# Block 0's first tiles multiplied by unnormalised x, rstd put in at emptying, and a new order of the first loads

## The chip, the cores and the metric

One core of a Trainium2 chip. The metric is the device time of one execution in microseconds, the median over runs. An execution has five engines at work: TensorE (PE), VectorE (DVE), ScalarE (ACT), GpSimd (POOL) and SyncE (SP), the last of which issues all DMAs here.

## The reference, cut to what matters

A layer takes 4096 prompt frames and 32 sample frames of width 1024, normalises each row, and projects it by W_in to 3584 columns. Two groups of 512 channels are made from the projection, both with causal convolutions along time, then mapped back by W_out and added to x.

```
hn   = x * rsqrt(mean(x * x) + 1e-6) * norm_g
proj = hn @ w_in                       # 1024 -> 3584
h, b, c, z, a, g, zb = split(proj)     # 512 columns each
out_a = b * conv3(c * h) * silu(z)
v     = a * sigmoid(g)
out_b = silu(layer_norm(conv31(v) + bias)) * silu(zb)
y     = rms_norm(x + concat(out_a, out_b) @ w_out)
```

rsqrt(...) is one number per row (frame), called rstd below. The frame is the column of a tile here, since the kernel keeps x transposed. Because rstd is a factor of the whole frame, it may stand before or after the product with W_in.

## The kernel before, in words

The frames are cut in 9 blocks of 460 columns (block 0 has 12 columns of padding and the sample's 32 frames in front). Every fp32 product is made of three: each operand is split in a high and a low part (fp32r), and high times high, high times low and low times high are added in PSUM (`split_product`, L1929; its matmuls are L1933 to L1935). A tile is 128 output channels by one block, 8 chunks of 128 input channels, so 24 matmuls.

The projection goes in 5 units of 14 periods. Unit 0 (periods 0 to 13) covers blocks 0 and 1 directly. Period n belongs to one pair of weight tiles (`ORDER`, L36): "ga" (sigmoid gate g and value a), "zz" (two tiles of zb), "hc", "bz". Its four tiles are t = 0, 1 for block 0 and t = 2, 3 for block 1. `FIRST_TILES` (L65) lists the first eight: periods 0 and 1 for block 0, then periods 0 and 1 for block 1, then period by period. Later units use a Strassen scheme for pairs of blocks, so in unit 0 the weights are also summed (POOL, `weight_sums`, L986), split, and written to HBM as forms.

What each engine does in unit 0:

- SP (L810 to L836): loads x of block 0 and 1, the gain norm_g, weight groups 0, 1 and 2; then in each period rows and x of block 2 and on (`load_row`, `load_st`), stores, weights of period n + 2 (`load_w`, L671), forms of period n + 1 (`store_forms`, L681). It issues in this order and waits in this order.
- ScalarE (L1339 to L1387): squares of x (`first_square`), mean square (`first_mean_square`), high parts of the weights (`weight_high`, L1214) and of x (`first_x_high`, L1230), and the evacuation of gate tiles through sigmoid or silu (`evacuate`, L1255) from PSUM to `sets`.
- VectorE (L1770 to L1797): sums the squares (`first_sums`, L1500), multiplies x by gain and rstd (`first_x_scale`, L1512, rstd read from PSUM), low parts of x and of weights (`first_x_low`, L1523; `weights_low`, L1531), then in each period some taps of the 31-tap convolution (`tap`, L1689), the emptying of the value tiles (`empty_banks`: `multiply_in` L1605, `gate_b` L1653), the low parts of the next weights, `finish`, more taps. The number of taps per period is a written-out quota (`tap_quota`, L150), 10 in most.
- TensorE (L2072 to L2087): mean squares as products with ones (`first_statistics`, L1939), the rstd spread over 128 partitions (`first_rstd`, L1947), ten warm-up matmuls, then the tiles. The first two tiles are made by halves (`standing_part`, L1961). Tile k uses PSUM bank k mod 6, and waits until tile k - 6 is emptied (`wait_evacuated`, L476).
- POOL (L1112 to L1126): rstd by a power (`x_row_rstd`, L951), then per period sums of weights and their low parts (`sums_low`, L1002).

```
            first_sums(0)
            first_sums(1)
            first_x_scale(0, range(HALF))
...
            for n in range(1, II):
                taps(TAPS_BEFORE[n])
                empty_banks(n - 1)
                if n + 1 < II:
                    weights_low(n + 1)
                finish(n - 1)
...
                taps(TAPS_AFTER[n])
```

## Time and profile before

| What | Before |
|---|---|
| median of 3 runs | 1566.16 us (1564.45 to 1568.77) |
| the profiled execution, its own time | 1561.36 us |
| span of its instructions | 1559.6 us |
| PE busy | 1537.6 us, 99% |
| DVE busy | 1262.9 us, 81% |
| ACT busy | 537.6 us, 34% |
| POOL busy | 578.4 us, 37% |
| DMA queue 1, share of 16 engines | 68.8% |

The span runs from the first to the last instruction of the program; the profiled execution's own time is 1.8 us longer. Times in a timeline are microseconds from the span's start. Each row of a timeline merges equal neighbours: start, time covered, engine, line, operation, output<-inputs, form, count, and in brackets how long the engine was idle before and who ended that. PEclk is the granted clock of TensorE as the records give it; they begin with the first change, so the column says 1.00 before that too.

### The profile page before, as it was taken

The numbers are of one execution on the slowest core, as the hardware profiler recorded it, in microseconds if no ns is written. First come the engines' busy times: TensorE is split into PE (matmuls) and PEld (weight loads), VectorE is DVE, ScalarE is ACT, GpSimd is POOL, SyncE is SP. The second block draws the span as 40 slices with busy tenths as digits, with TensorE's granted clock in tenths as the row PEclk, the third lists the DMA queues.
The fourth block names the chain that finished last, engine by engine and source line by source line (L and its number), as shares of the span: only waits on it lengthen the run. The fifth ranks groups of instructions, "written<-read, shape, count | busy, mean of one in ns | idle before, by whom it ended". The sixth has DMA issues, their size and how long they took to land. (4 is left out here: it accounts for less than half of the span.)

```text
span 1559.6 us, 19243 instructions
## 1 busy us (share of the span) xinstructions
PE 1537.6 (99%) x7244; PEld 1358.4 (87%) x7244; DVE 1262.9 (81%) x1175; ACT 537.6 (34%) x780; POOL 578.4 (37%) x494
## 2 busy tenths in 40 slices
PE   6999999999999999999999999999999999999998
PEld 6999999988888888888888888888898888888886
DVE  7699799998878998869798888789896677787853
ACT  5443433332242333332253312234533323323221
POOL 2766969112313121132221141146964233332320
PEclk9999999999999999999999999999999999999999
DMA  4987978788987789897779877757645433445441
GB/s 164 337 320 279 339 266 317 261 276 287 292 276 241 232 250 301 288 289 247 233 231 298 255 239 246 215 174 221 203 121 192 162 126 138 168 162 188 142 142 69
DMA packets 109648, 358.03 MB, mean 230 GB/s; under 512 B 16676, under 2 KB 20644, under 8 KB 105976
## 3 DMA queue, kind: packets, MB, share of 16 engines
q1 hardware_dynamic: 109560, 356.86, 68.8%
q8 instruction: 55, 0.90, 0.2%
q14 instruction: 33, 0.27, 0.0%
HBM read 263.02 MB, written 93.79 MB: 229 GB/s over the span
## 5 line engine op out<-in xcount | busy, mean ns | idle before, releaser
L1704 DVE SCALAR_TENSOR_TENSOR ps<-v,conv_b_taps,ps 128x920 f32<-128x920 f32 (+2 forms) x580 | 630.9, 1088 | 17.8
L1933 PE MATMUL ps<-xf,w_ring 128*128 128x460 f32 (+1 forms) x1624 | 602.8, 371 | 1.0 <-issue 0.8
L1935 PE MATMUL ps<-xf,w_ring 128*128 128x460 f32 (+1 forms) x1624 | 602.6, 371 | 0.0
L1934 PE MATMUL ps<-xf,w_ring 128*128 128x460 f32 (+1 forms) x1624 | 600.8, 370 | 0.0
L1933 PEld LDWEIGHTS ps<-xf,w_ring 128*128 128x128 f32 x1624 | 305.4, 188 | 35.2 <-issue 2.1
L1934 PEld LDWEIGHTS ps<-xf,w_ring 128*128 128x128 f32 x1624 | 305.4, 188 | 34.0
L1935 PEld LDWEIGHTS ps<-xf,w_ring 128*128 128x128 f32 x1624 | 304.9, 188 | 34.2
L1268 ACT ACTIVATE sets<-ps 128x460 f32<-128x460 f32 x168 | 92.9, 553 | 488.7 <-PE ps L1935 488.5
L1074 POOL TENSOR_TENSOR sets<-sets 128x460 f32<-128x460 f32 x42 | 56.2, 1337 | 414.9 <-ACT sets L1268 414.9
L1933 PE MATMUL ps<-w_out_split,mixed 128*128 128x512 f32 x528 | 206.0, 390 | 0.0
L1934 PE MATMUL ps<-w_out_split,mixed 128*128 128x512 f32 x528 | 205.7, 390 | 0.0
L1935 PE MATMUL ps<-w_out_split,mixed 128*128 128x512 f32 x528 | 205.5, 389 | 0.0
L1933 PEld LDWEIGHTS ps<-w_out_split,mixed 128*128 128x128 f32 x528 | 99.1, 188 | 21.2 <-DVE mixed L1765 0.5
L1935 PEld LDWEIGHTS ps<-w_out_split,mixed 128*128 128x128 f32 x528 | 99.1, 188 | 20.8
L1934 PEld LDWEIGHTS ps<-w_out_split,mixed 128*128 128x128 f32 x528 | 99.1, 188 | 20.5
L1477 ACT ACTIVATE ps<-h_rows 128x1024 f32<-128x1024 f32 x32 | 33.0, 1030 | 200.0 <-DVE h_rows L1851 200.0
L945 POOL TENSOR_TENSOR row_mean_sq_eps<-row_mean_sq,rms_eps 128x1 f32<-128x1 f32 x32 | 8.4, 264 | 228.4 <-ACT ps L1477 228.3
L1014 POOL TENSOR_TENSOR w_ring<-w_ring_f,w_ring 128x512 fp32r<-128x512 f32 x56 | 74.8, 1355 | 43.6 <-ACT w_ring L1228 43.6
L1933 PE MATMUL ps<-xf 128*128 128x448 f32 (+1 forms) x224 | 82.7, 369 | 0.0
L1935 PE MATMUL ps<-xf 128*128 128x448 f32 (+1 forms) x224 | 82.6, 369 | 0.0
L1934 PE MATMUL ps<-xf 128*128 128x448 f32 (+1 forms) x224 | 82.2, 367 | 0.0
L971 POOL TENSOR_TENSOR x_raw<-x_raw,rstd_spread 128x460 f32<-128x460 f32 x56 | 66.5, 1220 | 40.2 <-DMA rstd_spread<-rstd_spill 40.2
(166 smaller groups left out, 1650.2 us busy)
## 6 DMA issues: line engine op xcount, KB each, us to landing
w_ring<-weight_forms SPq DMA_DIRECT2D x294, 512.0 KB, 5.3
x_rows_again<-in_x_prompt SPq DMA_DIRECT2D x32, 512.0 KB, 4.3
out_y_prompt<-h_rows SPq DMA_DIRECT2D x32, 512.0 KB, 3.0
weight_forms<-xf SPq DMA_DIRECT2D x7, 2048.0 KB, 13.3
weight_forms<-w_ring SPq DMA_DIRECT2D x7, 2048.0 KB, 14.7
w_ring_f<-in_w_in SPq DMA_DIRECT2D x56, 256.0 KB, 3.1
xf_f<-in_w_in SPq DMA_DIRECT2D x26, 512.0 KB, 9.0
x_row<-in_x_prompt SPq DMA_DIRECT2D x28, 460.0 KB
```

The source lines that it names most:

```text
L945: pool.tensor_tensor(mean_sq[0:rows, r:r + 1], ssq[0:rows, r:r + 1], add, ALU.add).then_inc(h_ms, 1)
L971: pool.tensor_tensor(part, part, spread[:, 0:TB], ALU.mult).then_inc(x_scaled, 1)
L1014: pool.tensor_tensor(ring[:, slot, 1, :], ring_f32[:, slot, 1, :], ring[:, slot, 0, :].bitcast(F32), ALU.subtract).then_inc(late_lo, 1)
L1074: pool.tensor_tensor(sets[:, s, QC, :], sets[:, s, QC, :], sets[:, s, QD, :], ALU.add).then_inc(c22_made, 1)
L1268: act.activation(sets[:, n % 2, quarter, :], ps[:, bank, 0:TB], ACT.Copy).then_inc(copied, 1)
L1477: act.activation(out_pair(2)[0:rows, :], hrow[0:rows, s, :], ACT.Square, scale=RMS_SCALE, accum_out=ssq[0:rows, s:s + 1]).then_inc(h_sumsq, 1)
L1704: dve.scalar_tensor_tensor(dst, window, wb[:, j, k:k + 1], part, ALU.mult, ALU.add).then_inc(taps_done, 1)
L1933: pe.matmul(out, ahi, bhi, start=(start and x == 0), stop=False, skip_group_check=goes_on)
L1934: pe.matmul(out, ahi, blo, start=False, stop=False, skip_group_check=goes_on)
L1935: mm = pe.matmul(out, alo, bhi, start=False, stop=(stop and x == len(terms) - 1), skip_group_check=goes_on)
```

## The change

Block 0's x is no longer normalised before its first tiles. ScalarE makes the high part of x times gain (`raw_x_high`), VectorE the low part (`raw_x_low`), and the tiles (0,0), (0,1), (1,0) and (1,1) are multiplied with these. Block 1 is normalised first (`TURN` swaps the two blocks in the counts of the semaphores). The statistics of block 1 and its rstd come between the halves of the first two tiles, those of block 0 between the halves of tiles (0,2) and (0,3). Then ScalarE copies block 0's rstd from PSUM to `spread`, VectorE multiplies three tiles by it into `sets` (`raw_tile`), ScalarE applies sigmoid or silu in place (`gate_raw`), and the fourth, a's tile of period 0, gets it by a multiplication of its gate (`raw_gate`). After that block 0's x is scaled and split as before (`first_x_scale(0)`, `first_x_low(0)`), into the same buffers, for periods 2 to 13. The tiles (2,0) and (2,1) are made by halves. Squares of block 0 go to `sets` instead of a slot of `xf`. The first DMA is the gain; weight group 0 is loaded before block 1's x. POOL makes block 1's rstd, group 0's sums and low parts, block 0's rstd, then group 1's. The warm-up has 14 matmuls and starts when the first low part of x is there. Group 2's high and low weights are made before the loop over periods, and the emptying of period 0 too.

```diff
             def spread_rstd(w, b):
                 sp.wait_ge(rstd_out, 16 * stat_count(w, b))
+                if (w, b) == (1, 0):
+                    sp.wait_ge(x0_tiles, 3)
...
+            sp.dma_start(gain[:, :], A["norm_g"]).then_inc(gain_in, 16)
             for x in range(2):
                 src = A["xT"][0, :, x].rearrange("p (k t) -> p k t", t=TB)
                 sp.dma_start(st[:, x, :, :], src).then_inc(first_x_in[x], 16)
-            sp.dma_start(gain[:, :], A["norm_g"]).then_inc(gain_in, 16)
+            load_w(0)
             for x in range(2, 4):
...
-            load_w(0)
             load_w(1)
...
-            x_row_rstd(0, 1)
-            x_row_rstd(1, 2)
-            pool.wait_ge(x01_lo, 4)
+            x_row_rstd(1, TURN[1] + 1)
             weight_sums(0)
-            pool.wait_ge(x01_lo, 8)
             sums_low(0)
+            x_row_rstd(0, TURN[0] + 1)
             weight_sums(1)
...
+            def raw_x_high(k):
+                act.wait_ge(gain_in, 16)
+                act.wait_ge(first_x_in[k // HALF], 16)
+                act.activation(standing_x(0, 0, k, k + 1)[:, 0, :], st[:, k // HALF, k % HALF, :], ACT.Copy,
+                               scale=gain[:, k:k + 1]).then_inc(x0_raw_hi, 1)
+            def gate_raw(n, t):
+                part = sets[:, n, QUARTER[TILE_QUARTER[t]], PAD:TB]
+                act.wait_ge(x0_tiles, 2 * n + t + (1 if n == 0 else 0))
+                act.activation(part, part, FUNC[kind(n)]).then_inc(act_made, 1)
             def first_x_high(b, r):
-                act.wait_ge(x01_scaled, KC * b + 2 * r + 2)
+                act.wait_ge(x01_scaled, KC * TURN[b] + 2 * r + 2)
+                if b == 0:
+                    act.wait_ge(tile_done, TILE_AT[1, 1])
...
+            for k in range(6):
+                raw_x_high(k)
+            weight_high(0, 0)
+            raw_x_high(6)
+            raw_x_high(7)
+            weight_high(0, 1)
+            first_square(1, 0)
+            first_square(1, 1)
+            weight_high(1, 0)
+            weight_high(1, 1)
+            act.wait_ge(ready0, 7)
+            first_mean_square(1)
             first_square(0, 0)
             first_square(0, 1)
...
+            first_x_high(1, 0)
+            first_x_high(1, 1)
+            weight_high(0, 2)
+            first_x_high(1, 2)
+            weight_high(0, 3)
+            first_x_high(1, 3)
             first_mean_square(0)
...
+            act.wait_ge(first_spread, TURN[0] + 1)
+            act.activation(spread[:, 0:TB], ps[:, FIRST_BANK[0], 0:TB], ACT.Copy).then_inc(x0_rstd, 1)
+            gate_raw(0, 0)
             evacuate(0, 2)
+            gate_raw(1, 0)
+            gate_raw(1, 1)
+            weight_high(2, 0)
+            weight_high(2, 1)
             weight_high(1, 2)
             weight_high(1, 3)
+            for r in range(4):
+                first_x_high(0, r)
...
+            def raw_x_low(ks):
+                for k in ks:
+                    dve.wait_ge(x0_raw_hi, k + 1)
+                    dve.scalar_tensor_tensor(standing_x(0, 1, k, k + 1)[:, 0, :], st[:, k // HALF, k % HALF, :],
+                                             gain[:, k:k + 1], standing_x(0, 0, k, k + 1)[:, 0, :].bitcast(F32),
+                                             ALU.mult, ALU.subtract).then_inc(x0_raw_lo, 1)
+            def raw_tile(n, t):
+                dve.wait_ge(x0_rstd, 1)
+                dve.wait_ge(tile_done, TILE_AT[n, t])
+                dve.tensor_tensor(sets[:, n, QUARTER[TILE_QUARTER[t]], PAD:TB], ps[:, bank_of(n, t), PAD:TB],
+                                  spread[:, PAD:TB], ALU.mult).then_inc(x0_tiles, 1)
...
+            dve.wait_ge(gain_in, 16)
+            raw_x_low(range(6))
+            weights_low(0, [0])
+            raw_x_low(range(6, KC))
+            weights_low(0, [1])
+            first_sums(1)
+            weights_low(1)
+            first_x_scale(1, range(HALF))
+            first_x_low(1, range(2))
+            first_x_scale(1, range(HALF, KC))
+            first_x_low(1, range(2, 4))
             first_sums(0)
-            first_sums(1)
+            raw_tile(0, 0)
+            raw_tile(1, 0)
+            raw_tile(1, 1)
+            raw_gate()
+            dve.wait_ge(x0_gate, 1)
+            empty_banks(0)
+            weights_low(2)
             first_x_scale(0, range(HALF))
...
             for n in range(1, II):
                 taps(TAPS_BEFORE[n])
-                empty_banks(n - 1)
-                if n + 1 < II:
-                    weights_low(n + 1)
+                if n > 1:
+                    empty_banks(n - 1)
+                    if n + 1 < II:
+                        weights_low(n + 1)
                 finish(n - 1)
...
             pe.wait_ge(ready0, 7)
-            first_statistics(0)
-            first_rstd(0)
-            first_statistics(1)
-            for _ in range(10):
+            pe.wait_ge(x0_raw_lo, 1)
+            for _ in range(14):
                 pe.matmul(ps[:, 5, 0:P], ident[:, :], ident[:, :], start=True, stop=True)
...
+            by_halves(0, (0, 1), {2: (first_statistics, 1), 3: (first_rstd, 1)})
+            standing_tile(1, 0)
+            standing_tile(1, 1)
+            by_halves(0, (2, 3), {1: (first_statistics, 0), 2: (first_rstd, 0)})
+            standing_tile(1, 2)
+            standing_tile(1, 3)
+            by_halves(2, (0, 1), {})
+            for n, t in [(2, 2), (2, 3)] + [(n, t) for n in range(3, II) for t in range(4)]:
                 standing_tile(n, t)
```

## Rows read from the trace of the kernel before

**Rows 1.** The page's part on busy time: engine, busy us, share, instructions.

```profile
PE 1537.6 (99%) x7244; PEld 1358.4 (87%) x7244; DVE 1262.9 (81%) x1175; ACT 537.6 (34%) x780; POOL 578.4 (37%) x494
```

**Rows 2.** The timeline of TensorE, 0 to 28 us.

```profile
12.70 1.82 PE L1944 MATMUL ps<-ones,xf_f 128*115 128x1 f32 x8 [12.70 <-DVE xf_f L1510]
16.17 2.06 PE L1953 MATMUL ps<-ident,x_rstd_columns 115*128 115x115 f32 x8 [1.65 <-POOL x_rstd_columns L956]
18.02 1.69 PE L1944 MATMUL ps<-ones,w_ring_f 128*115 128x1 f32 x8
19.56 4.54 PE L2078 MATMUL ps<-ident 128*128 128x128 f32 x20
23.83 0.48 PE L1933 MATMUL ps<-xf 128*128 128x448 f32 x1
...
26.39 1.04 PE L1953 MATMUL ps<-ident,x_rstd_columns 115*128 115x115 f32 x8
27.20 0.45 PE L1933 MATMUL ps<-xf 128*128 128x448 f32 x1
```

**Rows 3.** The timeline of VectorE, 174 to 189 us.

```profile
174.21 0.58 DVE L1662 TENSOR_TENSOR conv_a_acc<-ps,conv_a_acc 128x416 f32<-128x416 f32 x1
...
187.73 0.64 DVE L1618 TENSOR_TENSOR v<-ps,sets 128x460 f32<-128x460 f32 x1 [6.25 <-ACT sets L1262]
```

**Rows 4.** L1933's products by stretch: stretch and length, PE busy (count), PEclk, DMA, GB/s.

```profile
23.80:84.10 60.30, 35.55 (x96) 1.00 0.70 260
...
23.80:177.90 154.10, 91.41 (x248) 1.00 0.79 290
```

**Rows 5.** The timeline of VectorE, the first 62 us.

```profile
7.34 1.12 DVE L1506 TENSOR_TENSOR xf_f<-xf_f 128x920 f32<-128x920 f32 x1 [7.34 <-ACT xf_f L1182]
...
18.32 2.51 DVE L1520 SCALAR_TENSOR_TENSOR x_raw<-x_raw,gain,ps 128x460 f32<-128x460 f32 x4 [1.28 <-PE ps L1953]
20.74 1.22 DVE L1534 TENSOR_TENSOR xf<-xf_f,xf 128x1024 fp32r<-128x1024 f32 x1
21.88 2.14 DVE L1526 TENSOR_TENSOR xf<-x_raw,xf 128x920 fp32r<-128x920 f32 x2
...
59.16 1.25 DVE L1701 TENSOR_SCALAR ps<-v,conv_b_taps,conv_b_bias_sb 128x938 f32<-128x938 f32 x1
```

**Rows 6.** VectorE's waits, 59.2 to 175 us: us in total, times, longest.

```profile
DVE w_ring L1534 <- ACT w_ring L1222: 1.1, 1, 1.1
```

**Rows 7.** The timeline of SP's DMA issues, 0 to 2 us and 57 to 65 us.

```profile
1.68 0.42 SPq L813 DMA_DIRECT2D gain<-in_norm_g  x1
...
57.84 1.06 SPq L641 DMA_DIRECT2D x_raw<-in_xT  x1
...
64.43 0.80 SPq L679 DMA_DIRECT2D xf_f<-in_w_in  x2
```

**Rows 8.** The timeline of ScalarE, the first 50 us and near 90 us.

```profile
5.57 1.74 ACT L1182 ACTIVATE xf_f<-x_raw 128x1840 f32<-128x1840 f32 x1 [3.54 <-DMA x_raw<-in_xT]
7.83 1.74 ACT L1182 ACTIVATE xf_f<-x_raw 128x1840 f32<-128x1840 f32 x1 [0.53 <-DMA x_raw<-in_xT]
...
14.78 1.99 ACT L1222 ACTIVATE xf<-xf_f 128x1024 fp32r<-128x1024 f32 x2
...
28.59 1.28 ACT L1262 ACT_TABLE_LOAD   x1
...
89.28 1.24 ACT L1201 ACTIVATE x_raw<-x_raw,gain 128x460 f32<-128x460 f32 x2
```

**Rows 9.** The timeline of POOL, the first 50 us.

```profile
14.96 1.15 POOL L956 TENSOR_TENSOR x_rstd_columns<-x_mean_square_eps,minus_half 115x4 f32<-115x4 f32 x1 [13.20 <-ACT x_mean_square_eps L1187]
...
42.13 4.77 POOL L1006 TENSOR_TENSOR xf<-xf_f,xf 128x1024 fp32r<-128x1024 f32 x2 [5.24 <-DVE xf L1526]
```

**Rows 10.** The timeline of VectorE at two places where POOL is at work.

```profile
76.37 3.49 DVE L1534 TENSOR_TENSOR w_ring<-xf_f,w_ring 128x1024 fp32r<-128x1024 f32 x2
...
159.08 5.30 DVE L1650 SCALAR_TENSOR_TENSOR conv_a_acc<-u,conv_a_taps,conv_a_acc 128x910 f32<-128x910 f32 x2
```

More of the change, by code:

```diff
@@ L373, in build_program @@
         first_spread = sem("first_rstd_spread")
+        x0_raw_hi = sem("x0_raw_hi")
+        x0_raw_lo = sem("x0_raw_lo")
+        x0_rstd = sem("x0_rstd_copied")
+        x0_tiles = sem("x0_tiles_times_rstd")
+        x0_gate = sem("x0_gate_times_rstd")
         x01_scaled = sem("x01_scaled")
@@ L989, in weight_sums @@
                 if g == 1:
-                    pool.wait_ge(first_stat, 2)
+                    pool.wait_ge(first_stat, TURN[1] + 1)
                 for f in range(2):
@@ L1514, in first_x_scale @@
                 dve.wait_ge(gain_in, 16)
-                dve.wait_ge(first_spread, b + 1)
+                dve.wait_ge(first_spread, TURN[b] + 1)
                 for k in ks:
@@ L1965, in standing_part @@
                 for r in rs:
-                    if n == 0:
-                        pe.wait_ge(x01_lo, 4 * b + r + 1)
+                    if n == 0 and b == 0:
+                        pe.wait_ge(x0_raw_lo, 2 * r + 2)
+                    elif (n, b) in ((0, 1), (2, 0)):
+                        pe.wait_ge(x01_lo, 4 * TURN[b] + r + 1)
                     terms = []
@@ L2072, in _, with by_halves @@
             pe.wait_ge(ready0, 7)
-            first_statistics(0)
-            first_rstd(0)
-            first_statistics(1)
-            for _ in range(10):
+            pe.wait_ge(x0_raw_lo, 1)
+            for _ in range(14):
                 pe.matmul(ps[:, 5, 0:P], ident[:, :], ident[:, :], start=True, stop=True)
-            for rs in (range(2), range(2, 4)):
-                for t in range(2):
-                    pe.wait_ge(w_lo_w, t + 1)
-                    standing_part(0, t, rs)
-                    if t == 0 and rs[0] == 0:
-                        first_rstd(1)
-            for n, t in FIRST_TILES[2:] + [(n, t) for n in range(2, II) for t in range(4)]:
+            def by_halves(n, ts, between):
+                for x, (rs, t) in enumerate((rs, t) for rs in (range(2), range(2, 4)) for t in ts):
+                    if t < 2:
+                        pe.wait_ge(w_lo_w, 2 * n + t + 1)
+                    if rs[0] == 0 and 4 * n + t >= 6:
+                        wait_evacuated(pe, *divmod(4 * n + t - 6, 4))
+                    standing_part(n, t, rs)
+                    if x in between:
+                        between[x][0](between[x][1])
+            by_halves(0, (0, 1), {2: (first_statistics, 1), 3: (first_rstd, 1)})
[6 more added lines that the diff above has]
+            for n, t in [(2, 2), (2, 3)] + [(n, t) for n in range(3, II) for t in range(4)]:
                 standing_tile(n, t)
```

49 lines of the change are left out of this document (15 added, 34 removed).

## The prediction

> **What bounds the kernel now.** I read the page's busy shares first, then TensorE's waits, then the four engines' timelines of the first 60 us, then how far TensorE had come at set times. TensorE is busy 99% of the span [rows 1]; the view of its waits lists four, and only the first is long: 12.7 us for the sums of block 0's squares. Two more stretches come before the first useful product: the rstd of block 0 (16.17 us) and ten warm-up products, 20 passes from 19.56 us. The first product of the projection starts at 23.83 us [rows 2]. From there TensorE runs on almost without a break, so the end moves by what TensorE's first product gains, less what is put between products, less every new stall. A lead at the start is worth something only if no other engine's deadline uses it up.
>
> The tightest deadline comes much later, on VectorE. A tile's PSUM bank is used again six tiles on, and for tile 1 of a period VectorE must have emptied it. In period 6 VectorE does that with L1662, ending at 174.8 us (174.21 + 0.58) [rows 3], and the 32nd tile, which waits for it, starts at 177.9: 248 of L1933's products, eight to a tile, had started by then [rows 4]. That is 3.1 us of room. Between its first tap at 59.16 us [rows 5] and 174.8 VectorE waits only 1.1 us for ScalarE at the weights of period 5 [rows 6]. So a late first tap stays late there, less at most 1.1 us.
>
> **The start.** norm_g's DMA goes first, 0.42 us of issue [rows 7], and x of block 0 lands that much later: ScalarE began on its halves at 5.57 and 7.83 us [rows 8], so now at 6.0 and 8.2. The two halves are 2.26 us apart for 920 KB, so a 512 KB weight tile costs 1.26: the first weights land at 9.5 and 10.7. Block 1's x slips behind them to 13.0 and 15.2.
>
> ScalarE multiplies x by gain at 0.57 us a chunk (two in 1.24, one 0.67 [rows 8]). VectorE has chunk 0's low part at 7.4, pitch 0.61 [rows 5]. Weight high takes 1.05 (the second of two is done 1.99 after the first begins), low 1.22 [rows 5, 8]: ready at 11.9, the second tile at 14.2. TensorE starts 14 warm-ups at 7.4; 20 passes took 19.56 to 23.83, 0.2135 each [rows 2], so 28 take 6.0 and end at 13.4. **First product: 13.4 us, against 23.83: 10.4 us earlier.** Nothing it needs is later than that.
>
> What moves in between products: two statistics and one more rstd. The rstd (8 passes) took 26.39 to 27.20 among products, against 1.85 from 16.17 to 18.02 in front of them [rows 2]. The statistics took 1.54 (18.02 to 19.56) in that slower stretch; among products between 0.8 and 1.5, I take 1.0, as it is of the rstd's kind. Together 2.8 us.
>
> The clock: before, the products' rate doubled just where the warm-ups ended, after TensorE had been at work from 16.17 on, 7.7 us; warm-up passes of 128 columns came every 0.2135 us, the rate of the lower level, 1.2 GHz, and the rstd at 26.39 took less than half of the first. Now 6.0 us of work stand ahead of the first product, so up to 1.7 us of products run at half rate: 0 to 0.9 us, I take 0.4. The Trainium skill (TensorE: Matmul & The Clock Gate, "What's actually happening") says that the lower level is the default and activity releases it; by it all of the second level's gain might come earlier or later than I say, which the rise just at 23.9 neither confirms nor refutes.
>
> **Chain to block 0's rstd.** A tile is 4.94 us (19 tiles in the 93.8 us between two counts [rows 4]), a half 2.47. TensorE: three halves to 20.8, statistics of block 1 (its sums are done at 20.0: two squares of 1.74 [rows 8], three adds of 1.12 and one half as wide, 0.6 [rows 5]), a half, rstd to 25.1 (POOL's power 1.15 [rows 9] is hidden by the half), two tiles of pair 1 to 34.9, two halves to 39.8. VectorE from 25.1: eight scalings 4.9 (four in 2.51), four low parts 4.3 (two in 2.14), 0.7 of waiting for ScalarE, sums of block 0 4.0 [rows 5]: 39.0 at best. POOL's sums of weight group 0, which now start when the rstd of block 1 is made (23.1), run beside these. Beside POOL two low parts took 3.49 where twice 1.22 is 2.44 [rows 10]; a meeting costs VectorE 1.05. I take two, 41.1. **TensorE stalls 1.4 us** (0 to 3). Statistics to 42.2, a half, rstd at 45.5, the last half to 48.0.
>
> ScalarE copies the rstd (0.6, near the 0.57 pitch of the gain), VectorE multiplies three tiles (0.58 each, as 416 columns took [rows 3]). ScalarE loads its table (1.28 [rows 8]) before the sigmoid, done at 47.9, so the tile that needs the bank, at 48.0, doesn't wait. VectorE: raw gate, v's three pieces to 49.8. ScalarE: a second table, two silus of 0.55 to 0.6 and weight group 2's first high part, 51.7. VectorE: two low parts of weights, 54.0; then block 0's real x, which before was done at 18 to 30 us, now lies here: eight scalings 4.9, four low parts 4.3, a cast. That is 63.3 with nobody in the way; POOL's low parts of group 1 (2.4 each [rows 9]) and sums of group 2 meet two of the four, 1.05 each and a little for the lengths. **First tap about 64.7 us, 5.5 us later than 59.16.** Bounds: with no meeting at all 61.8 (2.6 late, the stall gone too), with six meetings 68.2 (9 late).
>
> **What is queued behind the moved steps.** SP loads block 2's x into the same buffer and now waits for block 0's low parts, until about 64.6; before, that DMA went at 57.84 [rows 7]. Behind it stand the state's store, group 3's weights and group 2's forms. Group 3's weights went out at 64.43 before [rows 7], so they slip 1 to 2 us, less than VectorE's own 5.5. ScalarE in order: group 2's high parts moved ahead of the taps, nothing of TensorE behind them. POOL's rstd of block 0 ahead of group 1's sums costs 1.15, hidden by ScalarE's wait. The head's lead hides none of this.
>
> **The sum.** TensorE reaches period 2 at 57.9 plus about 1.5 of waiting for block 0's low parts, against 64.4 (84.1 less four tiles [rows 4]): some 5 us ahead. Then group 3's low weights, first at 77.6 (76.37 plus half of 3.49 [rows 10]), come 5.5 late, at 83.1, where TensorE stood at 84.1 before with its 13th tile [rows 4]: the lead is down to 1. In period 6 VectorE is 5.5 - 1.1 = 4.4 late and the room was 3.1: **+1.3 us** for everything after. Then VectorE waited 6.25 us of its own before, at 187.73 [rows 3], so its lateness ends there; TensorE's doesn't, since it has no idle time to give up. The profiled execution took 1561.36 us by the clock of the runs; 1.3 more is 1562.7. The median of the three runs shown is 4.8 above it, and the forecast is made against the median: 1566.16 + 1.3 = 1567.4. Bounds of the first tap (2.6 to 9 late) give -1.6 to +4.8. Below 0.3%, 4.7 us, a change can't be told from none.
>
> **Rivals.** (a) *The lead is kept*, 1559.2. TensorE ends 7 us earlier (10.4 - 2.8 - 0.4, as if no stall came). VectorE would have to be done in period 6 at least 3.9 us earlier than before, some 8 less than I have; for a gain over 4.7 it must be 1.6 early, some 6 less. For it: VectorE's ops with two inputs in SBUF are stretched by POOL in these periods (a pair of low parts by 1.05; two steps of group A's convolution took 5.30 where the first tap, a little wider, took 1.25 [rows 5, 10]): five pairs and two convolutions, some 11 us in all. If a late VectorE meets POOL idle, that goes. Against: ScalarE must split the same weights first, and POOL's low parts follow it at once, so the late VectorE meets those instead. 0.17.
>
> (b) *VectorE late enough to be slower*, 1572. The same port, the other way: six meetings in the first 65 us (9 late, +4.8), and one more in periods 2 to 6, +1.1. It decides from a first tap at about 68 us. For it: every low part of x and every add of squares now lies in POOL's busy time; the price of one is 1.05 [rows 10]. Against: scalings read PSUM and ran at 0.61 beside POOL. 0.17. The Trainium skill (SBUF - State Buffer, "Who interferes with whom") says that a VectorE instruction with two inputs in SBUF contends with a GpSimd one that reads SBUF, and that one blocks for the other's whole length; 3.49 for 2.44 is in that direction. By it a meeting with a POOL instruction of 2.4 could cost 2.4.
>
> (c) *The start doesn't come earlier*: weights or x held up behind each other so that the first product is at 18 or later. The time is the forecast's all the same, since VectorE decides; it has no chance of its own.
>
> **How the numbers follow.** Forecast 0.66, its own range 1564.5 to 1571; (a) 0.17; (b) 0.17. Faster 0.17, same 0.66, slower 0.17. The range for 8 in 10 reaches half into both rivals: 1560.5 to 1572.
>
> **What would show it.** Right: first product near 13.4, TensorE's products at full rate by 15; a wait of 1 to 2 us before block 0's statistics; first tap near 64.7; TensorE waiting a few us for group 3's low weights near 78 to 83, and again for VectorE's conv_a_acc or v pieces in periods 4 to 6; the 32nd tile near 179. Wrong: a first tap before 62 with no TensorE waits after 90 (then (a)), or one after 68, or waits of TensorE for DMA or ScalarE, which I have none of.

## The result, and the profile after

The changed kernel takes 1573.58 us (median of 6 runs, 1572.37 to 1575.81), the kernel before 1565.87 in the runs beside it: a ratio of 1.0051 with a 95% interval of 1.0038 to 1.0064. It is slower by 0.5%, where a change too small to be told from none was predicted (1567.4 us). Its profiled execution took 1573.64 us, with a span of 1571.9. That is 12.3 us more than the profiled span of before (1559.6), but that execution took 1561.36 us, 4.5 less than the median of 1565.87; by the medians the change costs 7.7.

The page's busy shares of the changed kernel, to be held against [rows 1]:

```profile
PE 1544.8 (98%) x7252; PEld 1362.2 (87%) x7252; DVE 1277.6 (81%) x1187; ACT 542.4 (35%) x789; POOL 569.3 (36%) x494
```

TensorE does eight matmuls more, all of them warm-ups, and is busy 7.2 us longer: work done at half clock, mostly. VectorE has twelve instructions more and 14.7 us more of busy time, of which the new instructions (eight low parts, three tiles and one gate) explain about half.

The view of TensorE's waits, those of 1 us and more (us in total, times, longest):

```profile
PE ps L2143 <- DVE xf L1566: 9.2, 1, 9.2
PE ps L1998 <- DVE w_ring L1586: 5.6, 1, 5.6
PE ps L1998 <- DVE xf L1558: 1.8, 2, 1.6
PE ps L1998 <- POOL mixed L1110: 1.1, 1, 1.1
PE ps L2009 <- DVE sets L1542: 1.1, 1, 1.1
```

The 12.7 us for block 0's squares became 9.2 for the first low part of x. The new long one is 5.6 us for the low part of a weight tile. TensorE's timeline shows where each comes:

```profile
9.24 6.26 PE L2143 MATMUL ps<-ident 128*128 128x128 f32 x28 [9.24 <-DVE xf L1566]
22.66 1.65 PE L2009 MATMUL ps<-ones,w_ring_f 128*115 128x1 f32 x8
26.70 1.04 PE L2018 MATMUL ps<-ident,x_rstd_columns 115*128 115x115 f32 x8
43.65 1.85 PE L2009 MATMUL ps<-ones,sets 128*115 128x1 f32 x8 [1.10 <-DVE sets L1542]
49.49 1.04 PE L2018 MATMUL ps<-ident,x_rstd_columns 115*128 115x115 f32 x8
91.08 0.74 PE L1998 MATMUL ps<-xf,w_ring 128*128 128x448 f32 x1 [5.64 <-DVE w_ring L1586]
```

The first product starts at 15.21 us, 8.6 earlier than the 23.83 of [rows 2]. The row at 91.08 is the first product of period 3; the products behind it start every 0.37 us, those of the kernel before there every 0.20. TensorE's clock is at its lower level there. The view by stretch (stretch and length, busy us with count for PE, PEld, DVE, ACT, POOL, then the granted clock):

```profile
40.00:47.00 7.00, 5.90 (x27) 5.14 (x26) 3.52 (x4) 0.26 (x1) 1.13 (x2) 0.93 1.00 425
47.00:49.00 2.00, 2.00 (x7) 1.74 (x6) 0.00 (x0) 0.00 (x0) 1.92 (x2) 0.50 0.80 328
49.00:60.00 11.00, 11.00 (x55) 9.64 (x55) 6.74 (x11) 8.98 (x11) 4.23 (x4) 0.98 0.01 4
91.00:98.00 7.00, 6.92 (x20) 6.17 (x21) 6.86 (x7) 3.65 (x6) 0.00 (x0) 0.55 0.80 253
98.00:110.00 12.00, 12.00 (x61) 10.95 (x60) 11.82 (x11) 5.04 (x6) 10.22 (x6) 1.00 0.85 350
```

The clock records of the trace show that it fell twice to 1.2 GHz: from 46.04 for 3.41 us, after a wait of 1.1 us and eight passes of one column; and from 90.41 for 6.83 us, 5.0 us into the wait of 5.64. The first fall cost 1.7 us: the half tile from 45.35 to 49.49 took 4.14 us, and the same products took 2.48 in the kernel before. The second cost 2.9 (the experiment a_fill, below).

VectorE's timeline from block 0's rstd to its first tap and near 90 us:

```profile
51.16 1.69 DVE L1574 TENSOR_TENSOR sets<-ps,rstd_spread 128x448 f32<-128x448 f32 x3 [7.57 <-ACT rstd_spread L1385]
...
59.09 2.50 DVE L1552 SCALAR_TENSOR_TENSOR x_raw<-x_raw,gain,ps 128x460 f32<-128x460 f32 x4
61.50 4.31 DVE L1558 TENSOR_TENSOR xf<-x_raw,xf 128x920 fp32r<-128x920 f32 x2
65.74 2.50 DVE L1552 SCALAR_TENSOR_TENSOR x_raw<-x_raw,gain,ps 128x460 f32<-128x460 f32 x4
68.16 3.29 DVE L1558 TENSOR_TENSOR xf<-x_raw,xf 128x920 fp32r<-128x920 f32 x2
71.37 1.31 DVE L1846 CAST mean_w<-mean_w_f 128x128 fp32r<-128x128 f32 x1
72.60 1.25 DVE L1753 TENSOR_SCALAR ps<-v,conv_b_taps,conv_b_bias_sb 128x938 f32<-128x938 f32 x1
...
84.99 4.91 DVE L1756 SCALAR_TENSOR_TENSOR ps<-v,conv_b_taps,ps 128x938 f32<-128x938 f32 x4
89.81 2.35 DVE L1586 TENSOR_TENSOR w_ring<-xf_f,w_ring 128x1024 fp32r<-128x1024 f32 x2
```

The first tap is at 72.60 us, 13.4 later than the 59.16 of [rows 5]. Group 3's low weights, at 76.37 before [rows 10], begin at 89.81, also 13.4 later. In POOL's timeline the low weights of group 1 lie beside the low parts of x:

```profile
58.81 4.99 POOL L1017 TENSOR_TENSOR w_ring<-w_ring_f,w_ring 128x1024 fp32r<-128x1024 f32 x2 [6.69 <-ACT w_ring L1231]
63.75 1.09 POOL L1037 COPY v<-hist_b 128x30 f32<-128x30 f32 x1
```

Where did the time go? I took the start of the same product in both traces (7,128 of them, counted in order) and call the difference to the first profile of before the shift, in us, negative for ahead:

| kernel | period 2 | period 3 | period 4 | unit 1 | unit 2 | unit 4 | output projection | end |
|---|---|---|---|---|---|---|---|---|
| the changed kernel | +0.5 | +6.9 | +9.8 | +9.8 | +9.5 | +9.6 | +11.6 | +12.3 |
| before_again | -0.6 | -0.6 | -0.6 | -0.6 | -0.8 | -0.8 | +0.5 | +1.2 |
| b_pad5 | +0.8 | +1.2 | +1.3 | +2.4 | +2.4 | +2.4 | +3.8 | +4.5 |
| b_pad11 | -0.7 | +6.3 | +8.1 | +8.1 | +8.0 | +11.7 | +12.5 | +13.2 |
| a_fill | -0.5 | +6.6 | +6.7 | +8.2 | +8.4 | +8.4 | +9.4 | +9.9 |
| a_no_x0 | -1.3 | -1.3 | -1.2 | +4.2 | +7.3 | +7.3 | +7.3 | +6.9 |
| a_quota | +0.9 | +1.5 | +1.5 | +6.2 | +7.1 | +7.1 | +7.1 | +7.1 |
| a_swap | -0.6 | 0.0 | +8.5 | +8.5 | +8.3 | +8.3 | +10.1 | +10.8 |
| a_pool | +3.0 | +7.9 | +10.0 | +10.1 | +9.9 | +9.9 | +11.3 | +11.9 |
| a_table | -0.9 | +5.5 | +8.0 | +8.0 | +7.3 | +10.2 | +12.3 | +12.9 |
| c_all | +1.9 | +1.9 | +1.9 | +7.0 | +9.0 | +9.0 | +10.6 | +11.3 |
| b_dma | +3.3 | +3.3 | +3.3 | +3.3 | +2.3 | +2.3 | +2.3 | +2.6 |
| c2 | -3.0 | -2.4 | -2.4 | -1.3 | -0.5 | -0.5 | +7.3 | +8.0 |
| c3 | -2.6 | -2.0 | -2.0 | 0.0 | +3.6 | +3.6 | +7.8 | +8.2 |
| c4 | -2.5 | -1.9 | -1.9 | -0.6 | +3.1 | +3.2 | +3.7 | +4.3 |
| a_catch | -0.2 | +0.4 | +0.4 | +1.3 | +4.8 | +4.8 | +8.8 | +9.2 |
| a_catch2 | -0.3 | +0.3 | +0.3 | +0.3 | +1.3 | +1.3 | +1.4 | +2.1 |
| c5 | -2.9 | -2.3 | -2.3 | -0.9 | +0.6 | +0.6 | +1.4 | +2.1 |
| c6 | -2.7 | -2.1 | -2.1 | -2.1 | +0.7 | +0.7 | +2.7 | +3.3 |

The first row tells the result. The lead of 8.6 us is gone at period 2; from there to period 4 the kernel loses 9.3 more, and then almost nothing up to the output projection.

### The profile page after: what moved, and what is told of

The parts are those of the page before. It is cut to its first block and busy times, and to the rows that moved or that the text cites. A ratio compares the mean times of both kernels' runs of the same rounds, so it can differ in the third digit from the quotient of the medians.

```text
span 1571.9 us, 19300 instructions
## 1 busy us (share of the span) xinstructions
PE 1544.8 (98%) x7252; PEld 1362.2 (87%) x7252; DVE 1277.6 (81%) x1187; ACT 542.4 (35%) x789; POOL 569.3 (36%) x494
```

## The experiments

My theory after the result: VectorE's first tap is 13.4 us late, and that alone sets the loss, through group 3's low weights and a clock fall behind that wait. Rivals: the new order of the loads, the clock falls by themselves, or other costs of the change further on.

### VectorE late in the kernel before: b_pad5, b_pad11, before_again

```diff
+            # just ahead of finish(n - 1) in period 1, so ahead of its taps, k times (k = 5 or 11)
+            dve.tensor_scalar(acc_ps[:, 0:2 * TB], xf[:, 3, 0:2, ...], 1.0, None, ALU.mult)
```

> The kernel before, unchanged, for a second profile of it, since its first profiled execution lay 4.5 us below its own median and the one after on its median. Both theories: the first product near 23.8 us, no wait of TensorE over 2 us after that, ratio 1.000. If the 12.3 us between the two profiles hold 4 us that come from one low profile, this profile's span is near 1563 and differs from the first one after unit 0.

> The kernel before, with 11 more VectorE instructions of about 1.2 us (920 columns, SBUF to PSUM) right before period 1's taps, so that its first taps come 13 us later, as in the changed kernel; nothing else moves. Theory V (VectorE's late taps decide): TensorE waits some 6 us for the low weights of period 3 and runs at the lower clock for some us after it, from there on 9 to 10 us behind; total +8 to +13 us against before. Rival S (what TensorE has between its products, and the clock dip near 46 us, decide): no more than +2 us, since none of that is in it. Rival Q (SP's queue, blocked by block 2's x until block 0's x is split, brings period 3's weights too late): no more than +3 us, since SP isn't blocked here.

> The kernel before with 5 instead of 11 added VectorE instructions of 1.2 us, so its first taps come 5.5 to 6 us late, which is what the prediction had taken for the change. Theory V: the prediction's own sum, no wait for period 3's low weights (6.5 us of room), a wait of 0 to 2 us in periods 4 to 6; the end of unit 0 at 0 to +2 us, ratio 1.000 to 1.001. Rival (VectorE's lateness is passed on one to one): +5 us.

Measured: before_again 1.0003 (0.9994 to 1.0013), b_pad11 1.0048 (1.0031 to 1.0065), b_pad5 1.0008 (0.9996 to 1.0019). With eleven instructions the first tap is at 71.9 us, and TensorE's waits show the row of the changed kernel again:

```profile
71.92 1.26 DVE L1710 TENSOR_SCALAR ps<-v,conv_b_taps,conv_b_bias_sb 128x938 f32<-128x938 f32 x1
```

```profile
PE ps L1944 <- DVE w_ring L1543: 6.8, 1, 6.8
```

The clock falls during that wait, from 87.3 for 6.8 us. So the kernel before, with none of the change in it, loses 6.9 us by the medians once VectorE is 12.8 us late, where the changed kernel loses 7.7. Of the +13.2 at the end of its profile, 3.7 belong to neither: they come in unit 2, behind a wait of 1.9 us for ScalarE and a clock fall at 671.0, and this profiled execution lay 3.1 us above its median. With five the first tap is at 64.9, 5.8 us late, and TensorE is +2.4 after unit 0. That is nearly the case I predicted (first tap 64.7, +1.3).

### One part at a time: a_fill, a_table, a_pool, a_no_x0, b_dma

```diff
# a_fill: ahead of tile (3,0)
+    wait_evacuated(pe, 1, 2)
+    for _ in range(26): pe.matmul(ps[:, bank_of(3, 0), 0:P], ident, ident, start=True, stop=True)
# a_table: ahead of ScalarE's first raw_x_high
+    act.wait_ge(ready0, 7); act.activation(ssq[:, 0:1], ones[:, :], ACT.Copy)
# a_pool: POOL's group 1 sums ahead of block 0's rstd (and ScalarE's high parts for them earlier)
-    x_row_rstd(0, TURN[0] + 1)
     weight_sums(1)
+    x_row_rstd(0, TURN[0] + 1)
# a_no_x0: block 0's x stays unnormalised for periods 2 to 13
-    first_x_high(0, r); first_x_scale(0); first_x_low(0)
# b_dma: the kernel before with the new order of the first loads
+    sp.dma_start(gain, norm_g); (x of block 0); load_w(0); (x of block 1); load_w(1)
```

> The changed kernel with 26 warm-up products (52 passes of 128 columns, some 5.5 us at the full clock) on TensorE between the last tile of period 2 and the wait for period 3's low weights, so that TensorE has work in the 5.6 us in which it waited. Theory V with the clock as a second step: the low weights of period 3 come at 91.0 us as before, but the clock doesn't fall at 90.4, and the products of (3,0) aren't at half rate for 6.8 us: 2.9 us faster than the changed kernel at the end of unit 0 (9.8 late becomes 6.9 late). Rival (the low clock costs nothing, since VectorE is late anyway): the same end of unit 0, with a wait of 3 us in periods 4 to 6 in its place.

> The changed kernel with one tiny ScalarE copy (128x1) ahead of the wait for x, so that the table load (1.28 us, from 6.32 in the changed kernel) lies in the time in which the DMA is under way. Theory V: the first product at 13.9 us instead of 15.2, everything up to the first taps 1.3 us earlier (71.3), the end of unit 0 1 to 1.3 us earlier. Rival (weights, not x, set the start): the first product moves by less than 0.5 us.

> The changed kernel with POOL's sums of group 1 ahead of its rstd of block 0, and ScalarE's high parts of those sums ahead of block 0's mean square, so that POOL and ScalarE use the time in which they stood idle (38.7 to 45.9 us and 37 to 45.5). Theory P (POOL's chain holds the first taps back as soon as VectorE is a little earlier, by the edges of v at 64.8): edges at some 52 to 55 us instead of 64.8, POOL's sums of group 2 earlier; VectorE meets POOL less while it splits block 0's x (7.6 us for four low parts, 4.3 alone) and its first tap comes 2 to 4 us earlier, 69 to 71; 2 to 4 us faster at the end of unit 0. Theory V alone: POOL's order changes nothing but the meetings: -1 to +2 us. The sums of block 0's squares may meet POOL now: 1 to 2 us later statistics.

> The changed kernel without the later scaling and splitting of block 0's x (periods 2 to 13 are multiplied by the unnormalised x of block 0; that part of the result is left out), VectorE's 13.5 us for it fall away. Theory V: the first taps at 59 to 60 us instead of 72.6, no wait for period 3's low weights, one clock dip less; TensorE between -2 and +1 us against before at the end of unit 0, that is 9 to 12 us faster than the changed kernel. Rival S: the dip near 46 us and the statistics stay, so it stays slower than before by more than 3 us. Rival Q: faster too, since SP is free; not told apart here.

> The kernel before with the new order of the first loads alone (gain, x of block 0, weight group 0, x of block 1). Nothing in it uses the earlier weights. VectorE sums block 1's squares before it scales block 0's x, and those squares come 2.9 us later, so: the first product 2 to 3 us later than 23.8 us, the end of unit 0 +1 to +3 us (TensorE itself late, VectorE has its 11 us gap before the taps), ratio 1.001 to 1.002. Rival (the new order gives something by itself): no later than before.

- a_fill, 1.0038 (1.0022 to 1.0053): TensorE is kept at work while it waits, and the view by stretch shows 36 products where the changed kernel has 20:

```profile
91.00:98.00 7.00, 7.00 (x36) 6.44 (x36) 6.82 (x7) 3.79 (x6) 0.00 (x0) 1.00 0.80 269
```

  Between period 3 and 4 it loses 0.1 us instead of 2.9. So the second clock fall costs 2.9. Of that 1.5 came back by unit 1, with a wait of 1.2 for conv_a_acc, because VectorE was still as late.
- a_table, 1.0019 (1.0005 to 1.0032): the first product at 13.92 instead of 15.21. ScalarE's table load (1.28 us) no longer stands behind the wait for x, but this pair of traces doesn't show its price: x landed later here, so the warm-ups began only 0.4 us earlier, and the other 0.9 is a clock that rose at 12.97 instead of 15.32. All the profiles together do: the warm-ups begin at 9.1 to 9.6 in the eight without the copy, at 8.1 to 8.8 in the seven with it, 1.2 us earlier in the mean. Its profiled execution was 3.6 us above its own median.
- a_pool, 1.0058 (1.0041 to 1.0076), a miss: the sums of block 0's squares now met POOL, the wait before the statistics grew from 1.1 to 5.2 us, and the clock fell for 6.8 us. The first tap came at 73.0, where 69 to 71 was expected.
- a_no_x0, 1.0032 (1.0016 to 1.0048), leaves out the later normalising and splitting of block 0's x. It missed too: -2 to +1 us was expected at the end of unit 0, +4.2 measured. But it is 1.2 us ahead at period 4, with the statistics and the first clock fall still in it, so these alone don't make the kernel late. The first tap only came down to 64.0, because another holder was behind the one taken away:

```profile
64.03 1.26 DVE L1751 TENSOR_SCALAR ps<-v,conv_b_taps,conv_b_bias_sb 128x938 f32<-128x938 f32 x1 [2.63 <-POOL v L1039]
```

  It waited for v's edges, which POOL writes behind group 1's low weights. There was no wait for weights any more, yet waits of 3.0 for conv_a_acc and 1.5 for v came in periods 4 to 7, and the shift rose by 5.4 us.
- b_dma, 1.0015 (1.0005 to 1.0026): in the kernel before, the new order of the loads costs some 2 us. It doesn't explain 7.7.

### Fewer early taps: a_quota, a_swap, c_all, c2

```diff
 def tap_quota(n):
+    if n in Q: return Q[n]
# a_quota Q = {1: 2}; a_swap {1: 2, 2: 18}; c_all {1: 4}; c2 {1: 2, 2: 8, 4: 7, 6: 7}
# c2 and c_all also: a_table's copy, the cast of mean_w right after first_sums(0), and
+    pe.wait_ge(x01_scaled, 8)
+    for _ in range(5): pe.matmul(ps[:, FIRST_BANK[1], 0:P], ident, ident, ...)   # before first_statistics(0)
# c_all also a_pool's order
```

> The changed kernel with 2 taps in period 1 instead of 10; the eight go to period 7, where VectorE had a gap. Theory V: the low weights of period 3 are ready 9.6 us earlier, at 81 to 82 us, before TensorE asks for them at 85.4; no wait, no clock dip; 8 to 10 us faster than the changed kernel, within 1.5 us of before. Rival Q: the weights themselves still arrive as in the changed kernel (ScalarE has their high part at 80.7), so it isn't the weights if the wait goes; under Q the wait would stay at 4 us or more. Rival S: at most 3 us faster than the changed kernel.

> The changed kernel with 2 taps in period 1 and 18 in period 2: the same number by the end of period 2, but eight of them behind period 3's low weights and not ahead. Theory V in full (VectorE has one late sequence, and each of its deadlines passes the lateness on in turn): the low weights of period 3 at 82 us, no wait for them; then TensorE waits about 4 us at the 16th tile for VectorE's u pieces of period 2 (at 104 to 105 us, as in the changed kernel); the end of unit 0 at +4 to +7 us against before. Rival (only the wait for the low weights and the clock dip behind it cost anything): the end of unit 0 at +0.5 to +1.5.

> The changed kernel with all of it: the table load early, POOL and ScalarE reordered as in a_pool, five warm-up products in the place of the 1.1 us wait ahead of block 0's statistics, the cast of the mean weights moved into VectorE's idle 7 us, and 4 taps in period 1 instead of 10. Theories V and P together: no clock dip at 46 us (1.7 us), first product 1.3 us earlier, first tap at 64 to 66 us, no wait for period 3's low weights, waits of at most 2 us for VectorE in periods 3 to 6; the end of unit 0 between -3 and +1 us against before. If only single stretches are moved from one wait to the next, as with the smaller quota alone, it stays at +4 us or more.

> The changed kernel with POOL's order as it is, the table load early, five warm-up products ahead of block 0's statistics, the cast moved, and taps of unit 0 cut to 2, 8, 10, 7, 10, 7 in periods 1 to 6; the 16 go to period 7 and to unit 4, where quotas weren't used up. Theory V: VectorE has 19 us less to do before its deadline in period 6 and keeps ahead of TensorE in periods 3 to 6; first product at 13.9 us, no clock dip at 46 us if the five products do their work, the end of unit 0 between -3 and 0 us against before, ratio 0.998 to 1.000. If VectorE meets POOL again in the way that took back the relief in the kernel with the smaller quota, +2 to +4 us.

The taps are VectorE's work that nobody waits for at once, and they stand ahead of the low weights. Taking eight out of period 1 (a_quota, 1.0055, 1.0038 to 1.0073) removed the wait for the weights: +1.5 at period 3. But it was to end within 1.5 us of before and ended at +7.1, for the lateness was handed on:

```profile
PE ps L2000 <- DVE conv_a_acc L1716: 2.3, 1, 2.3
PE ps L2000 <- DVE v L1668: 1.9, 1, 1.9
```

a_swap (1.0055, 1.0038 to 1.0073) made the same eight in period 2, and TensorE waited 6.9 us for u one period later. c_all (1.0059, 1.0040 to 1.0078) missed as a_pool did, with a wait of 4.1 us before the statistics and waits of 2.5 for v and 2.0 for conv_a_acc behind it. c2 (1.0044, 1.0027 to 1.0061) spread the relief over periods 1 to 6, and TensorE stayed 2.4 to 0.5 us ahead from period 3 to unit 4. Then it lost 6.4 us (from -0.3 just ahead of it to +6.1) in one place, the layer norm of unit 4, and 1.2 more near 1186 us (see below). The place in c2:

```profile
1146.02 1.87 PE L2132 MATMUL ps<-ones,ln_tmp_b_f 128*128 128x1 f32 x8 [3.81 <-DVE ln_tmp_b_f L1783]
```

That wait is 0.7 us in the kernel before:

```profile
PE ps L2061 <- DVE ln_tmp_b_f L1727: 0.7, 1, 0.7
```

By the plan of the quotas c2 still owes eight taps up to period 55, and makes seven of them in period 56. VectorE was 5.7 us late there (a first tap at 1125.32 instead of 1119.63), TensorE waited 3.8 us, and during that wait, at 1144.3, the clock fell for 6.8 us.

### The same taps, paid back elsewhere: c3, c4, a_catch, c5, c6, a_catch2

```diff
# a_catch, a_catch2: quotas only, on the changed kernel. The others: c2's other edits too
# c3, a_catch   Q = {1: 2, 2: 8, 4: 7, 6: 7, and 11 in 8 to 12 and 15 to 17}
# c4            Q = {1: 1, 2: 7, 3: 9, 4: 7, 6: 7, and 11 in 8 to 12 and 15 to 20}
# c5            Q = {1: 1, 2: 7, 3: 9, 4: 7, 6: 7, and 11 in 16 to 26}
# c6, a_catch2  Q = {1: 2, 2: 8, 3: 9, 4: 7, 6: 7, and 11 in 17 to 25}
```

> The kernel of the change with the same help as c2 (a tiny ScalarE copy ahead of the first loads, five TensorE filler products before the statistics, the cast of the mean weights moved up, and 2, 8, 10, 7, 10, 7 taps in periods 1 to 6), but the 8 taps that c2 still owed until unit 4 are made in periods 8 to 17, 11 taps in each instead of 10. Theory: c2 kept TensorE ahead of the kernel before by 0.3 us up to the end of unit 4's first 14 groups, and lost 7.3 us at one place, where VectorE came 5.7 us late to the layer norm because of the taps owed: a wait of 3.8 and a clock fall of 6.8 us at half. Paid back earlier, this place should look as in the kernel before (wait 0.7, no clock fall), and the end should be 0 to +2 us against the kernel before in the profile, ratio 0.9995 to 1.0015. Rival: the loss after unit 0 belongs to the change itself and comes back elsewhere: end +6 or more, ratio 1.004.

> As c3, with 1, 7, 9, 7, 10, 7 taps in periods 1 to 6 and the debt of up to 11 taps paid back in periods 8 to 20. Theory: the wait of 0.9 us for v in period 5 goes too, TensorE stays 2 to 3 us ahead through unit 0, and the end is -2 to +1 us against the kernel before, ratio 0.998 to 1.001. Rival: a wait for v or conv_a_acc comes elsewhere in units 0 or 1 and takes it: end +3 or more.

> The kernel of the change with c3's quotas of taps alone (2, 8, 10, 7, 10, 7 in periods 1 to 6, paid back in periods 8 to 17), nothing else changed. Theory: the taps put off remove the wait for the low weights and most later waits; what is left is the start, TensorE level with the kernel before at period 2 instead of 3 us ahead: end +2 to +5 us, ratio 1.001 to 1.003, so that of the change's loss of 8 us by the medians more than half was the taps' order. Rival: taps are not what holds VectorE: end +7 or more as in a_quota, ratio 1.005.

c3 1.0018 (1.0006 to 1.0030), c4 1.0018 (1.0003 to 1.0032), a_catch 1.0027 (1.0014 to 1.0040). The wait at the layer norm of unit 4 went back to the 0.7 us of before or less, as the theory has it. But by the profiles the ends are +8.2 and +9.2 in c3 and a_catch where I expected 2 and 5 at most, and +4.3 in c4 where I expected 1. Two other places took it. The first is the start of unit 1, where VectorE splits x. The timeline of VectorE in the kernel before, then in c4:

```profile
300.45 2.07 DVE L1562 TENSOR_TENSOR xf<-xf_f,xf 128x1840 fp32r<-128x1840 f32 x1
```

```profile
303.62 2.07 DVE L1618 TENSOR_TENSOR xf<-xf_f,xf 128x1840 fp32r<-128x1840 f32 x1
```

VectorE is 3.2 us late with it, by the taps paid back in periods 8 to 12; in c5, which makes none there, it begins at 301.09. TensorE's next product in c4:

```profile
305.79 0.45 PE L2002 MATMUL ps<-xf,w_ring 128*128 128x460 f32 x1 [2.25 <-issue]
```

It starts 0.1 us after VectorE's part ends (305.69). The view names no releaser, but that is the one instruction that ends there. The clock fell at 307.0 for 3.4 us. Together the shift goes from -0.6 to +3.1.

The second place is the split of the output projection's input near 1186 us, in c3 and a_catch but not in c4. The wait of TensorE in c3, and POOL's instruction in c3, then in c4:

```profile
PE ps L2002 <- POOL mixed L1112: 3.2, 1, 3.2
```

```profile
1185.83 6.60 POOL L1112 TENSOR_TENSOR mixed<-mixed_f,mixed 128x2048 fp32r<-128x2048 f32 x1
```

```profile
1183.69 4.62 POOL L1112 TENSOR_TENSOR mixed<-mixed_f,mixed 128x2048 fp32r<-128x2048 f32 x1
```

VectorE's add of conv_b and mixed_f beside it, in c3, then in c4:

```profile
1185.30 2.73 DVE L1815 TENSOR_TENSOR conv_b<-conv_b,mixed_f 128x2048 f32<-128x2048 f32 x1
```

```profile
1185.68 4.78 DVE L1815 TENSOR_TENSOR conv_b<-conv_b,mixed_f 128x2048 f32<-128x2048 f32 x1
```

In c3 POOL started 0.5 us after VectorE's add and took 2 us more; in c4 POOL was first, and VectorE's add took 4.8 instead of 2.7. In these two traces TensorE waits 3.2 us where VectorE was first and 0.3 where POOL was. By the medians c3 and c4 are level (1568.37 and 1568.83 us), so the 3.9 us between their profiled ends don't show in the timed runs.

> As c4 (1, 7, 9, 7, 10, 7 taps in periods 1 to 6), but the taps owed are made in periods 16 to 26, none before unit 1 begins. Theory: c3 and c4 lost 3.6 to 3.7 us where unit 1 starts, because the taps paid back in periods 8 to 12 made VectorE 3.2 us late with unit 1's x (it ended 305.69 instead of 302.52 us, and TensorE started at 305.79 after 2.2 us without work), and a clock fall of 3.4 us followed. Without taps there TensorE stays 1 to 2 us ahead through units 0 to 4; the end is -2 to +1 us against the kernel before in the profile, and up to 4 us more where POOL's mixed split meets VectorE near 1186 us (c3 and a_catch; 1.1 us of it is in the kernel before's second profile too). Ratio 0.9985 to 1.0005. Rival: VectorE has no room in unit 1 either, and the taps only move the wait to periods 16 to 28: end +3 or more, ratio 1.002.

> As c5 with one tap more in period 1 and in period 2 (2, 8, 9, 7, 10, 7) and the nine taps owed made in periods 17 to 25. Theory: as c5 within 1 us, ratio 0.9985 to 1.0005; a wait of about 1 us for v in period 5 may be there as in c2. Rival as for c5.

> The kernel of the change with c6's quotas alone. Theory: TensorE 0 to +1.5 us against the kernel before from period 3 on to unit 4 (a_catch had +0.4 to +1.3 in unit 0, then +4.8 from the start of unit 1), end +1 to +2.5, up to 4 more with the meeting near 1186 us; ratio 1.0005 to 1.002. Rival: the wait moves into unit 1: as a_catch, +4.8 at unit 2, ratio 1.0027.

c5 takes 1564.29 us, 0.9997 of before (0.9987 to 1.0008); c6 1.0004 (0.9993 to 1.0015); a_catch2 1565.99 us, 1.0013 (1.0003 to 1.0022). The clock didn't fall in c5 and c6 ahead of the last 6 us, and c5 has no wait over 1.2 us behind the one of 1.6 for block 0's low parts at period 2. Its profile ends at +2.1, where I expected 1 at most: the 3 us of lead that it had at period 2 were lost around the start of unit 1. So with the same change, a few numbers of taps per period take 1.0051 to 1.0013. With the three small edits at the start on top of the same numbers, c6 is level with the kernel before, and so is c5. No version beat it.

## Why the prediction was wrong

**The mechanism was right, and so was its warning.** The forecast said that a lead at the start is worth something only if no other deadline uses it up, that VectorE's late taps would be handed to group 3's low weights, and rival (b) said "It decides from a first tap at about 68 us". The first tap came at 72.60. b_pad5 and b_pad11 confirm the two ends of that scale, 1.0008 and 1.0048. That rival (b)'s 1572 lies near the measured 1573.58 is in part luck: it had 9 us of lateness, with everything above the forecast from meetings of VectorE with POOL, and no clock fall. Of the 7.9 us beyond my 5.5, 5.0 came ahead of block 0's rstd and from other causes, and a clock fall came on top.

**The term that failed is the first tap: 5.5 us late by the sum, 13.4 measured, beyond my upper bound of 9.** By its parts:
- First product 13.4 predicted, 15.21 measured: 1.8. The warm-ups began at 9.24 instead of 7.4, because ScalarE's table load stood behind the wait for x (6.32, 1.28 us long). In the kernel before it ran at 0.75, ahead of the wait, and I had counted it only before the sigmoid.
- Statistics at 1.0 each, measured 1.51 and 1.70 from their start to that of the next product: 1.2 in all. I took less than the row's 1.54, on the ground that passes among products are quicker; those of the statistics weren't. The rstd at 0.8 was right, 0.81 and 0.82 by the same measure; the end of the last one counts, and comes 0.2 later.
- The clock: I priced the start (0.4, in the rival's sum and not in this chain) and no fall in the middle. At the start no product ran at half rate, the records show full clock from 15.3. At 46 us it fell and cost 1.7. Where a statistic of one-column passes follows a short wait, I had no row for it. The Trainium skill (TensorE: Matmul & The Clock Gate, "What's actually happening") says that the lower level is the default and activity releases it. The falls here agree: 1.1 us of waiting and eight one-column passes went ahead of the first, 5.0 us of waiting ahead of the second.
- The stall before the statistics: 1.4 predicted, 1.1 measured. The products between the two rstds took 0.3 more than my tiles of 4.94. Together these make 1.8 + 1.2 + 0.2 + 1.7 - 0.3 + 0.3 = 4.9; block 0's rstd ended at 50.5 instead of 45.5.
- From there to the first tap 22.1 us instead of 19.2. By my own terms it should have been 19.9: 63.3 and two meetings at 1.05 make 65.4, not 64.7. Two of the four low parts of x took 4.31 where two alone took 2.14 [rows 5], the other two 3.29, and the cast 1.31 where it took 0.22 before. The meetings with POOL thus cost 3.3 instead of 2.1, and the cast 1.1 more. The Trainium skill (SBUF — State Buffer, "Who interferes with whom") lets VectorE instructions with at most one SBUF input pass, outside the modes that use both ports; the trace agrees: the four scalings beside POOL at 59.09 took 2.50, as alone.

What was mis-sized in that last part is the flat 1.05 for a meeting. POOL's two rows beside the low parts and the cast:

```profile
68.30 2.18 POOL L1009 TENSOR_TENSOR xf_f<-xf_f 128x512 f32<-128x512 f32 x1
```

```profile
70.55 2.05 POOL L1011 TENSOR_TENSOR xf_f<-xf_f 128x512 f32<-128x512 f32 x1
```

In each meeting the later instruction ends about as long after the earlier one's end as it takes by itself, or less. The low part that began at 61.50 ended 1.0 us after POOL's at 63.80, the one at 69.28 ended 1.0 after POOL's at 70.47, and the cast at 71.37 ended 0.1 after POOL's at 72.60. So a meeting costs about what was left of the other's instruction: 2.2, 1.1 and 1.1 us here, with 2.3, 1.2 and 1.2 left.

**Then the prediction's own arithmetic held.** Group 3's first low part was ready at 91.0 instead of 77.6, and the room to TensorE's need at 84.1 was 6.5: 13.4 less 6.5 is 6.9, and the shift at period 3 is +6.9. (The 77.6 is the end of the first of the two instructions at 76.37, which took 1.27; half of the pair's 3.49, as I wrote, would give 78.1.) What I had not was the clock fall behind that wait, 2.9 by a_fill. The deadline in period 6 took nothing more: TensorE itself was 9.8 late by then, and VectorE 9.9 (184.10 against 174.21 [rows 3]). VectorE won back 3.5 us where I had 1.1. 1.1 is the wait for ScalarE, which was gone as forecast; the rest came of meetings with POOL won and lost, as rival (a) had it in kind. Among them: group 3's low weights took 2.35 instead of 3.49, and the two steps of group A's convolution 2.38 instead of 5.30 [rows 10], with POOL idle beside them, but the low weights just ahead of these took 6.73 instead of 4.35.

**The lead at period 2.** Predicted 5 us, measured -0.5: 8.6 at the first product, less 1.6 for the statistics and rstd of block 1, 5.7 for wait, statistics, rstd and clock fall of block 0, and 1.8 of waiting for the low parts of x (predicted 1.5).

**SP's queue.** Block 2's x went at 71.47 instead of 57.84 [rows 7], so group 3's weights slipped by 8.2 us (72.62 against 64.43) where I had 1 to 2. It cost nothing: ScalarE had their high parts at 80.8, nine us before VectorE came to them. I had no wait of TensorE for DMA or ScalarE, and the view shows none.

**What stays open.** In the profile the changed kernel loses 2.7 us more behind unit 4's start. before_again loses 2.0 there too, most of it between 1180 and 1200 us: there VectorE's add beside POOL's split took 6.0 us, as in the changed kernel, instead of the 4.5 of the first profile. c3 and c4 show that 3 us can hang on which engine comes first there. That this makes up the whole difference between 12.3 by the profiles and 7.7 by the medians was only argued. a_quota's profile was 2.8 us under its median, so how much of its gain in unit 0 the timed runs keep is open too. How the last 2 us of a_catch2 divide between table load, clock fall and loads was not separated; c6, with the same numbers of taps, took the first two away. The new numbers of taps weren't run in the kernel before, so whether they are worth something there too isn't shown. And the first product itself moves from execution to execution: at 14.4 to 15.6 us in the eight profiles that start like the changed kernel.

## What to carry to other kernels

A lead won at the start can be lost again at the next deadlines of another engine. Find the engine whose work was moved behind the start, add up how late it gets, and subtract the room at each later deadline, the first of them above all. Price each meeting of VectorE with GpSimd by what is left of the other's instruction, and not by one number. When that engine is late, look in its queue for work that nobody waits for (here ten taps ahead of two low weights): putting that off took the ratio from 1.0051 to 1.0013, but the debt must be paid back where the engine has room. Carried to the next busy place it cost nearly as much as before (c2, 1.0044). A wait of a few microseconds on TensorE can bring a clock fall that costs half as much again.

## What the runs showed of the hardware

- The granted clock fell around quite short stops of TensorE: after 1.1 us of waiting and 1.85 us of one-column passes (half level for 3.4 us); 1.2 us behind a wait of 2.25 in c4; 0.4 behind one of 2.1 in c3, and 1.5 behind one of 3.15 there; 1.2 behind one of 4.1 in c_all (3.4 us each). During waits of 3.8 in c2, 5.6 in the changed kernel and 6.8 in b_pad11 it fell for 6.8 us each. After waits of 2.0 in a_catch, 2.3 in a_quota and 2.5 in c_all it did not fall.
- At the start the clock rose at another moment in each execution: 2.9 us (c2) to 6.1 us (the changed kernel) after the first warm-up, whose passes are the same.
- One VectorE pair of 128x920 adds costs 2.14 us alone, 3.29 and 4.31 beside POOL; the cast of 128x128 0.22 in the kernel before and 1.31 beside POOL. The one that starts first keeps its time or nearly, and the other waits for its end: POOL's 128x2048 split took 4.62 when it was first and 6.60 when it was second, VectorE's 128x2048 add 4.78 when second and 2.73 when first.
- A tiny ScalarE copy ahead of the first wait brings the table load forward, from 6.3 us to 0.75; the warm-ups that wait for ScalarE's first high part then begin 1.2 us earlier in the mean of the profiles (9.1 to 9.6 without it, 8.1 to 8.8 with it).
